# Attention probabilities turned once and multiplied with V in one fp32 product, and the two maps of the differential heads combined before the turn

## The reference

```python
oa = rms_norm(gqa_axial(ua, ...), g_out_a)        # A: 2 shared key/value heads, rotary angles
ob = rms_norm(mla(ub, ...), g_out_b)              # B: low-rank queries, keys and values
oc = diff_attention(uc, ...)                      # C: two softmax maps for each head
od = rms_norm(neighbourhood_attention(ud, ...))   # D: local windows with a relative bias
mix = concatenate([oa, ob, oc, od]) @ w_out
```

```python
p = softmax(sc)                      # sc: two maps, each with scores q.k * scale + bias
a = p[:, :, 0] - lam * p[:, :, 1]
o = a @ v
```

## Time and profile before

| | before |
|---|---|
| median of 3 runs | 3702.86 us (3701.55 to 3702.9) |
| span of the profiled execution | 3702.0 us |
| TensorE busy | 3240.0 us, 88% |
| VectorE busy | 1533.5 us, 41% |
| ScalarE busy | 1345.0 us, 36% |
| GpSimd busy | 590.2 us, 16% |
| first layer: attention A | from 119.0 to 223.1 |
| attention C, twice | from 268.9 to 363.2, and from 409.6 |
| attention D, twice | from 550.0 to 590.2, and from 635.4 |
| attention B | from 774.2 to 892.3 |

### The profile page before, as it was taken

The page is one execution under the profiler, slowest core; times in us unless marked ns, Lnnn a source line. Parts: engine busy times, 40 slices in busy tenths (PEclk is TensorE's granted clock), DMA queues, the critical chain, the costliest instruction groups (busy, mean ns, idle before and its releaser), DMA issues. The chain is left out here.

```text
span 3702.0 us, 41905 instructions
## 1 busy us (share of the span) xinstructions
PE 3240.0 (88%) x16432; PEld 2703.9 (73%) x16432; DVE 1533.5 (41%) x1889; ACT 1345.0 (36%) x2198; POOL 590.2 (16%) x275
## 2 busy tenths in 40 slices
PE   6788988887859999999769889888859699999996
PEld 5777777676748888888658778776757588888885
DVE  4848554377152111111358467443771611111115
ACT  3647644365132121212227466443640421212113
POOL 1000000111222222222210000002022222222222
PEclk9889998888879999999879999998979799999997
DMA  6030222100131111111230311221001311111112
GB/s 147 1 75 9 67 63 63 31 11 6 46 125 46 46 51 45 50 46 45 102 63 1 74 34 40 63 62 42 1 12 40 131 52 46 46 49 47 45 51 102
DMA packets 264655, 192.24 MB, mean 52 GB/s; under 512 B 64392, under 2 KB 245384, under 8 KB 264458
## 3 DMA queue, kind: packets, MB, share of 16 engines
q1 hardware_dynamic: 264510, 190.42, 19.1%
q10 hardware_dynamic: 12, 0.02, 0.0%
HBM read 142.17 MB, written 24.89 MB: 45 GB/s over the span
## 5 line engine op out<-in xcount | busy, mean ns | idle before, releaser
L240 POOL TENSOR_TENSOR w_l_m<-w_raw_m,w_h_m 128x1024 fp32r<-128x1024 f32 (+2 forms) x136 | 313.7, 2307 | 1101.1 <-ACT w_h_m L231 1100.9
L248 PE MATMUL u_ps<-h_hi,w_h_m 128*128 128x512 f32 x1024 | 406.8, 397 | 14.6 <-POOL w_l_m L240 14.6
L249 PE MATMUL u_ps<-h_lo,w_h_m 128*128 128x512 f32 x1024 | 407.2, 398 | 0.0
L249 PE MATMUL u_ps<-up_l,w_h_m 128*128 128x512 f32 x1024 | 398.4, 389 | 0.0
L248 PE MATMUL u_ps<-up_h,w_h_m 128*128 128x512 f32 x1024 | 398.4, 389 | 0.0
L231 ACT ACTIVATE w_h_m<-w_raw_m 128x1024 fp32r<-128x1024 f32 (+2 forms) x136 | 135.8, 1003 | 578.0 <-PE u_ps L252 562.6
L1614 DVE TENSOR_TENSOR mlp_out_t<-mlp_out_t,u_ps 128x1024 f32<-128x1024 f32 x64 | 78.1, 1221 | 591.8 <-PE u_ps L252 591.8
L252 PE MATMUL u_ps<-h_hi,w_l_m 128*128 128x512 f32 x1024 | 323.1, 397 | 0.0
L252 PE MATMUL u_ps<-up_h,w_l_m 128*128 128x512 f32 x1024 | 315.3, 389 | 0.0
L1604 DVE TENSOR_TENSOR m_square<-m_relu 128x1024 f32<-128x1024 f32 x64 | 78.4, 1225 | 512.8 <-ACT m_relu L1590 512.8
L248 PEld LDWEIGHTS u_ps<-h_hi,w_h_m 128*128 128x128 f32 x1024 | 193.8, 189 | 61.7 <-POOL w_l_m L240 15.4
(11 more groups left out here) (301 smaller groups left out, 6756.7 us busy)
## 6 DMA issues: line engine op xcount, KB each, us to landing
w_raw_m<-in_w_down SPq DMA_DIRECT2D x64, 512.0 KB, 4.1
w_raw_m<-in_w_up SPq DMA_DIRECT2D x56, 512.0 KB, 4.1
x_mlp_pre<-out_x SPq DMA_DIRECT2D x16, 512.0 KB, 8.9
out_x<-x_mlp_pre SPq DMA_DIRECT2D x16, 512.0 KB, 2.6
x_mlp_post<-out_x SPq DMA_DIRECT2D x16, 512.0 KB, 8.8
out_x<-x_mlp_post SPq DMA_DIRECT2D x16, 512.0 KB, 2.6
w_raw_o<-in_w_out SPq DMA_DIRECT2D x14, 512.0 KB, 4.2
x_mix_pre<-in_x SPq DMA_DIRECT2D x8, 512.0 KB, 8.2
```

Of the source, the lines that this page charges most:

```text
L240: last = nc.gpsimd.tensor_tensor(lo[0:rows, u % 2, cols, :], raw[0:rows, u % 2, cols, :], hi[0:rows, u % 2, cols, :], ALU.subtract)
L248: nc.tensor.matmul(o, w_hi, x_hi[:, tok], start=first, stop=False)
L249: nc.tensor.matmul(o, w_hi, x_lo[:, tok], start=False, stop=False)
```

## The change

In A, B and D the turned block is copied once as plain float32 (`pt`), each piece by one engine: ScalarE takes the first and VectorE the second piece of a tile in A and B, in D ScalarE the even and VectorE the odd tiles. The value product has the turned block as stationary operand and streams the 64 columns of V in float32, so its result has queries on the partitions, and there is no `ot`, no fold and no low half of V. TensorE's order is `scores(n + 2)`, `turn(n)`, `values(n - 1)`. `o_ps` has two slots.

In C a new `difference_stage` takes both maps of a head together, `n` counting query tiles (16 in a stage). VectorE computes `ratio = lam * z0 / z1`, with `lam` the negative of the reference's. GpSimd scales the second map by it and adds it to the first. Only the sum is turned and multiplied with V, and `divide` multiplies with `1 / z0`. Both maps' scores of a tile go to one slot each.

```diff
-                    def values(g, half):
...
-                            for j, pt in enumerate((pt_h, pt_l)):
-                                last = nc.tensor.matmul(ot_ps[:, cols], v[:, k, :],
-                                                        pt[:, g % 2, k - base_of[i // 2], cols],
...
-                    def finish(g):
...
+                    def values(n):
+                        m, i = n // NT, n % NT
+                        first, cnt = tiles[i][0:2]
+                        if taken(n, "act"):
+                            pe.wait_ge(S["pt_act"], taken(n, "act"))
+                        if taken(n, "dve"):
+                            pe.wait_ge(S["pt_dve"], taken(n, "dve"))
...
+                        for k in range(cnt):
+                            last = nc.tensor.matmul(o_ps[:, m % 2, i, :], pt[:, n % 2, k * P:(k + 1) * P],
+                                                    maps[m][2][:, first + k, :], start=(k == 0), stop=(k == cnt - 1))
+                        last.then_inc(S["pv_done"], 1)
...
-                    for n in range(n_all + 3):
+                    for n in range(n_all + 1):
                         if n + 2 < n_all:
                             scores(n + 2)
                         if n < n_all:
                             turn(n)
...
+                        if n >= 1:
+                            values(n - 1)
```

The new stage for C, cut to its waits and to the orders of TensorE, ScalarE, GpSimd and VectorE, one behind the other (the exponentials, maxima and value products are written as above):

```diff
+        def difference_stage(maps, bias, mix_cols, mix, lam):
+            pieces = evacuations(tiles, n_all, lambda n, b: "dve" if b == 1 and n % 2 == 1 else "act")
+                prob = sb(c, "prob_c", [P, 3, 2, SEQ])
...
+                    def scores(n, r):
+                        if n >= 1:
+                            pe.wait_ge(S["exp_done"], 2 * n + r - 1)
...
+                    def turn(n):
+                        pe.wait_ge(S["combined"], n + 1)
+                        for p, (of, k0, k1, who, count) in enumerate(pieces):
...
+                            if p >= 2:
+                                pe.wait_ge(S["pt_act" if pieces[p - 2][3] == "act" else "pt_dve"], pieces[p - 2][4])
...
+                    for n in range(n_all + 3):
+                        if 2 <= n < n_all + 2:
+                            turn(n - 2)
+                        if n + 1 < n_all:
+                            scores(n + 1, 0)
+                            scores(n + 1, 1)
+                        if n >= 3:
+                            values(n - 3)
...
+                    for n in range(n_all + 2):
+                        if n + 1 < n_all:
+                            exponential(n + 1, 0)
+                        if n >= 2:
+                            lift(n - 2)
+                        if n + 1 < n_all:
+                            exponential(n + 1, 1)
...
+                    for n in range(n_all):
+                        pool.wait_ge(S["ratio_done"], n + 1)
+                        nc.gpsimd.tensor_scalar(prob[:, n % 3, 1, :], prob[:, n % 3, 1, :], ratio[:, 1, n:n + 1], 1.0,
+                                                ALU.mult, ALU.mult).then_inc(S["scaled"], 1)
+                        pool.wait_ge(S["scaled"], n + 1)
+                        nc.gpsimd.tensor_tensor(prob[:, n % 3, 0, :], prob[:, n % 3, 0, :], prob[:, n % 3, 1, :],
+                                                ALU.add).then_inc(S["combined"], 1)
...
+                    for n in range(n_all + 4):
+                        if n + 1 < n_all:
+                            maximum(n + 1, 0)
+                        if n < n_all:
+                            weigh(n)
+                        if n + 1 < n_all:
+                            maximum(n + 1, 1)
+                        if 2 <= n < n_all + 2:
+                            lift(n - 2)
```

V's low half goes in all preparations, for instance in `pair_stage`:

```diff
-                            for n in range(2):
-                                dve.wait_ge(S["tt_hi"], n + 1)
-                                nc.vector.tensor_tensor(v_half(n, HD, P), turned(n), v_half(n, 0, HD), ALU.subtract)
```

More of the change, by code:

```diff
@@ L427, in norm_stage, with evacuations @@
             end_stage()
-        def attention_stage(tag, maps, tiles, mix_cols, mix, combine=None):
+        def evacuations(tiles, n_all, taker):
+            out_, count = [], {"act": 0, "dve": 0}
+            for n in range(n_all):
+                cnt = tiles[n % NT][1]
+                for b, k0 in enumerate(range(0, cnt, 4)):
+                    who = taker(n, b)
+                    count[who] += 1
+                    out_.append((n, k0, min(cnt, k0 + 4), who, count[who]))
+            return out_
@@ L442, in attention_stage @@
+        def attention_stage(tag, maps, tiles, mix_cols, mix, taker):
             n_all = len(maps) * NT
-            n_groups = n_all // 2
             kmax = max(t[1] for t in tiles)
[L446 to L453, removed]
@@ L473, in attention_stage @@
[L473 to L484, removed]
+                o_ps = ps(c, f"o_ps_{tag}", [P, 2, NT, HD])
@@ L486, in _, with taken @@
+                def taken(n, who):
+                    return sum(1 for piece in pieces if piece[0] <= n and piece[3] == who)
                 @block.tensor
@@ L510, in turn @@
                                 .then_inc(S["ptr_done"], 1)
-                    def values(g, half):
[L513 to L521, removed]
-                            for j, pt in enumerate((pt_h, pt_l)):
-                                last = nc.tensor.matmul(ot_ps[:, cols], v[:, k, :],
-                                                        pt[:, g % 2, k - base_of[i // 2], cols],
-                                                        start=(at == 0 and j == 0),
-                                                        stop=(at == len(steps) - 1 and j == 1))
-                        if half == 1:
-                            last.then_inc(S["pv_done"], 1)
@@ L611, in maximum, with lift @@
                                                            accum_out=nmax[:, n:n + 1]).then_inc(S["max_done"], 1)
[L613 to L621 removed]
+                    def lift(n):
+                        if n >= 2:
+                            dve.wait_ge(S["pv_done"], n - 1)
+                        for p, (of, k0, k1, who, count) in enumerate(pieces):
+                            if of == n and who == "dve":
+                                dve.wait_ge(S["ptr_done"], p + 1)
+                                nc.vector.tensor_copy(pt[:, n % 2, k0 * P:k1 * P], t_ps[:, p % 2, 0:(k1 - k0) * P]) \
+                                    .then_inc(S["pt_dve"], 1)
@@ L641, in _ @@
+                        nc.vector.tensor_tensor(mix[:, :, mix_cols(m)], o_ps[:, m % 2, :, :],
+                                                zm.unsqueeze(2).to_broadcast([P, NT, HD]), ALU.mult) \
+                            .then_inc(S["map_done"], 1)
                     maximum(0)
                     maximum(1)
-                    for n in range(n_all + 4):
+                    for n in range(n_all + 3):
                         if n + 2 < n_all:
@@ L938, in _ @@
                                 act.wait_ge(S["tt_done"], n + 1)
[L939 removed]
+                                nc.scalar.activation(v_half(n), turned(n), ACT.Copy)
                         @block.vector
@@ L1085, in build @@
                              for i in range(NT)]
-                    attention_stage("d", maps, tiles, lambda m: bass.ds(pair * P + (12 * HD + m * HD), HD), mix)
+                    attention_stage("d", maps, tiles, lambda m: bass.ds(pair * P + (12 * HD + m * HD), HD), mix,
+                                    lambda n, b: "dve" if n % 2 else "act")
                 with ExitStack() as cb:
```

260 lines of the change are left out of this document (147 added, 113 removed).

## The result

| | before | after |
|---|---|---|
| median of 6 runs each, same chip | 3702.88 us (3698.01 to 3706.69) | 3711.61 us (3708.88 to 3719.53) |
| span of the profiled execution | 3702.0 | 3709.3 |
| attention A, two layers | 109.1, 107.5 | 123.5, 123.2 |
| attention B | 137.1, 137.1 | 154.4, 154.5 |
| attention C, four stages | 100.6, 100.4, 99.6, 100.2 | 91.0, 90.6, 93.2, 90.9 |

The ratio is 1.0027 with a 95% interval of 1.0016 to 1.0039: slower, by little more than what can be told. A and B grew by 64.9 us, C fell by 35.1, D by 10.5, the preparations by 8.5, and the rest by 3.3 (nearly all of it between attention B of the second layer and the end). That is the 7.3 us between the two spans; the medians are 8.7 apart.

The account below looks back on a forecast made before the run. TensorE was taken to bound A and B alone, C with VectorE, and mostly D. Terms of +70 (A, B), -3 (D), -40 (C) and -11 (preparations) gave +16, so 3720 us; range 3696 to 3756.

Parts of the forecast that it names:

- own range: Whole kernel: 3702 to 3738 us around the main case of 3720, which had chance 0.65.
- 0.103 us per pass: Value products in A, B and D: at this price the changed kernel would be faster by over 0.2%.
- A and B, +70 predicted: Attention A and B: 16 fp32 passes of 0.112 us add 0.62 us per tile, +17.5 per stage, +70 in two layers.
- those before the last turns: End of an A or B stage: waits of 0.2 to 0.3 us before the last turns go, 1.0 us.
- D, -3 predicted: Attention D: +3.2 us of passes per stage against saved waits and tail; -0.8 per stage, -3 in four.
- C, -40 predicted: Attention C: 32 tiles become 16 pairs, a stage falls from 94.4 to 84.5 us; -9.9 each, -40 in four.
- The loop that I named: Attention C: turn, scores, maximum, exponential, ScalarE's copy, back to the turn; 4.70 us a pair, 4.75 with the second copy.
- The 1.0 us for a later clock: Attention C, per stage: added because TensorE works little in the head and its clock may rise later.
- the 1.25 taken: Attention C: time in us assumed for GpSimd's scaling of the second map, between 1.04 and 2.45.
- The preparations, -11 predicted: Stages preparing attention: V's low half goes, 5.8 us in C and D, 1.8 a layer in B, 0.9 in A.
- Cheap passes: Rival in A, B and D: loads hidden under earlier passes, 0.056 us each, 3573 us; chance of 0.106 or less 0.12.
- GpSimd binding C: Rival in C: scaling at 2.45 us or more, 5.0 to 5.3 a pair, 3736 to 3756 us; chance 0.15.

Follow-up runs that it names:

- experiment 3: Changed kernel with only every second key block in the value product of A and B: 3597.0 us, ratio 0.9720 to the kernel before.
- experiment 1: Each half of the change alone, against the kernel before: only C changed 3689.3 us; only A, B and D changed 3763.3 us.
- experiment 4: Changed kernel with, in C, ScalarE's copy moved ahead: 3678.8 us; TensorE's order altered too: 3667.5; instead a second GpSimd scaling per pair: 3726.7.

## Why the prediction was right, and where its terms were off

The predicted 3720 was 8 us above the measured 3711.6, which lies in the range and in the own range. The sign and both large terms came from the mechanisms that were named. That the sum is so close is in part luck: against the table its terms are off by -5 (A and B), -7.5 (D), +5 (C) and +2.5 (the preparations), and 3.3 us fell where it had no term. (At 0.103 us per pass its sum gives 3696, 0.18% under before and not over 0.2%.)

- **A and B, +70 predicted, +65 measured.** The pass of 0.112 us is confirmed by the loads and by experiment 3, the tile is longer by 0.61 us (0.62). B is +17.4 in both layers (17.5). A is +14.4 and +15.7. The waits inside the stage, 1.15 of 90 us, went as well, and I had counted only those before the last turns. In the first layer the low clock at A's head is shorter too, 3.1 us and not 9.4 (a mean of 0.92 there against the 0.57 of the earlier trace rows). In the second it is as short in both kernels. The kernel of experiment 1 with A, B and D alone tells what that is worth: its first A has 9.6 us of low clock and takes 125.7 where this one takes 123.5. So with the clock alike A is +16.6, and 2.2 us of what is missing is the clock, for which the prediction had no term.
- **D, -3 predicted, -10.5 measured.** This is the term that was mis-sized: I took -0.8 a stage between bounds of -3 and +3, and it is -2.6. All of TensorE's waits for the split went, not half. Before, in the first D stage:

```profile
PE t_ps_d L292 <- DVE pt_l_d L620: 2.2, 5, 0.8
...
PE ot_ps_d L523 <- DVE pt_l_d L620: 0.8, 1, 0.8
PE o_ps_d L536 <- ACT ot_d L570: 0.5, 1, 0.5
```

That is 3.5 us, and after there are none behind the first exponential. The low clock at the head, 6.8 us before, is 3.4. In the D stages of other kernels here that have the new code and 6.2 to 6.7 us of low clock at their head, the stage is 43.2 to 43.6 and the gain 1.8 to 2.2, so some 0.6 of the 2.6 goes to the clock.
- **C, -40 predicted, -35 measured.** The loop that I named binds: 4.73 and 4.84 in turn, 4.78 a pair (4.70 to 4.75), with the wait before the turn for ScalarE's copy. Three stages are -9.3 to -9.8 (-9.9). The third is only -6.3: its low clock lasts until 25 us into the stage, where the others have 14 to 17 in all. The 1.0 us for a later clock was too little there. The table flatters this term: it counts up to the next projection, where the forecast counted up to the last write of mix. Up to that write the stages were 94.3, 93.9, 94.3 and 94.0 and are 85.8, 85.5, 87.9 and 85.9 (84.5), so -31.4 and not -40. The other 3.7 us lie behind the write, where the old C of experiment 1 lost 2.9 as well, so they are not shown to be the new stage's. In the first stage the head is right (10.4 of 10.5); the pairs under the low clock, 6.0 and 5.4, cost 1.8 and not 1.0, each of the others is 0.03 longer, and the end behind the last turn takes 5.7 and not 5.2.
- **GpSimd.** Its scaling takes 1.12 us, between the 1.04 and 2.45 of the bounds and close to the 1.25 taken. The estimate of 0.85 us from the Trainium skill ("GPSIMD Engine Reference", Engine selection) is too low by a quarter; by either there was room, and experiment 4 measured it.
- **The preparations, -11 predicted, -8.5 measured:** -3.5 in C, -3.4 in D, -1.3 in B, -0.4 in A.
- **The rivals.** Cheap passes: no, the distance is 0.112. The Trainium skill's rule for weight loads ("TensorE: Matmul & The Clock Gate", LDWEIGHTS (loading the stationary operand)) gives 0.107: it lies 0.005 below the measurement, 13 us on 2624 passes; the measurement decides. GpSimd binding C: no. A clock of 0.5 through C: no, 0.97 from 300 to 372; but the head showed that the mechanism is there, and it was worth more than the 1.0 us that I gave it.

One thing more was luck. The MLP loop could have stood at a place in the code at which its instructions are fetched in each round, as in both halves of the change, and the result would have been 9 to 28 us higher (3763.3 less 3754.6, 3689.3 less 3661.3) by no step of mine; the prediction had no term and no rival for it.

## What to carry to other kernels

Price a matmul with few streamed columns by its weight loads, and an fp32 one by two of them (0.112 us each here). In A and B, where TensorE was the bound, swapping the operands so that the result needs no turn cost more than the fold that it saved; in D, where TensorE also waited for the split, the same swap made the stage shorter. When a new stage is bound by a loop over two engines, look for an operation in it that stands behind another only by the order written; moving it in two lines was worth 33 us here. Before a difference of some tenths of a per cent is put down to an edit, compare the stages that the edit doesn't touch, and the packets in the queue for instructions.

## What the runs showed of the hardware beyond that

- A loop of 1564 instructions on TensorE ran without a fetch from the second round on when it began at 17, 29, 34, 62, 106 or 110 from a multiple of 256, and with a stop of 1 to 3 us and nine packets of 16 KB in each later round at 209 and 219. Three stops of 2.3 to 3.0 us are 8 of the 11 to 13 us that the MLP products grew by at 219. The clock is low for 8 to 11 us more in a layer than in the kernel before; at the two paces of a projection's products (0.43 and 0.235 us apart) that is 4 to 5 us, the rest. Where between these values it turns is not measured.
- 64 semaphore increments on TensorE ahead of the first barrier put off its first matmul by 6.2 us and its first projection by 7.1.
- In the head of C, with TensorE waiting for exponentials between its products (busy 4.5 of 8 us, then 6.2 of 8), the clock stayed at 1.2 GHz for 20 us. With the pauses partly filled by turns of a constant (6.6 of the first 8) it was at 2.4 GHz from 3.0 to 3.4 us on in three of the four stages, from 5.8 in the other.
